# A decoder layer in float32: the token-wise projection cut into 264 and 512 columns instead of three times 256

## The chip, the cores and the metric

One core of one Trainium2 chip runs the whole layer in one launch. The metric is the device time of the launch in microseconds (us); lower is better. The median of three runs before the change is 2868.61 us.

## The reference

One layer of a hybrid decoder for 2048 tokens of width 1024, cut to what the change touches:

```python
mod = silu(c) @ ada_w + ada_b            # shift1, scale1, gate1, shift2, scale2, gate2
h = rms_norm(x) * (1 + scale1) + shift1
proj = h @ w_in                          # q 512 | k 128 | v 128 | deltanet q,k,v 1536 | beta 4 | decay 4 | z 512 | gates 2048
q, k = rope(rms_norm(q)), rope(rms_norm(k)); o_attn = sliding_window_attention(q, k, v, sinks)   # window 128
dq, dk, dv = silu(causal_conv(deltanet_qkv))                                                     # 4 taps, 12 x 128 channels
beta, g = sigmoid(beta), -exp(a_log) * softplus(decay + dt_bias)
o_dn = gated_delta_rule(l2norm(dq), l2norm(dk), dv, g, beta)                                      # then norm and silu(z)
x = x + gate1 * ((sigmoid(gA) * (o_attn @ wA) + sigmoid(gD) * (o_dn @ wD)) @ w_out)
x = x + gate2 * swiglu(rms_norm(x) * (1 + scale2) + shift2)
```

## The kernel before

The tokens are worked on in four blocks of 512 (`b` = 0 to 3); the feed-forward part runs after block 1 and after block 3 for two blocks at once. Every float32 product is made of three matmuls in the type fp32r: both operands are split into a high and a low part, and hi x hi, lo x hi and hi x lo are summed in one PSUM bank. ScalarE (ACT) makes the high part of the weights (`w_hi`, line 1074), VectorE (DVE) the low one (`w_lo`, line 1616). Both of them work through `split(b, u)`, unit of weights after unit, over a ring of three buffers, so a unit can't be split before TensorE (PE) has done with the unit three places earlier. A unit is 128 x 1024 values.

Each engine executes a sequence that is written out by hand; nothing is scheduled by a program. Semaphores tie the sequences together. Within a block the sequences run through these stages:

- *Channels.* Twelve units (`U_DN`) give the 12 x 128 deltanet channels with the weights standing and 512 tokens streaming (`by_feature`, line 2457, 24 matmuls of 512 columns). For each channel ACT empties the bank (line 1232), DVE runs the four taps (lines 1963 to 1968), ACT applies silu (line 1257). DVE's step for channel `c` is: split the unit two channels ahead, wait for the bank, four taps. Strength and decay (beta, decay; 8 columns) come from `by_group` (line 2467) after channels 0 and 1: 32 columns of plain float32 weights, laid over the four column groups of the array, so that the result lies in features by tokens and must be turned by four more matmuls with `gather8` (line 2591). `gates_1` to `gates_4` on DVE make the gates out of them during channels 2, 4, 6 and 10. In block 0 the two first channels are made while the norm delivers `h` one slice of 128 features at a time.
- *Token stage.* Queries, keys and values (768 columns) are made with tokens as the standing operand and the weights streaming, in three groups of 256 columns (`by_token`, line 2487), each in two half units. Between them, for each of the four token tiles `t`, PE runs `turn_features(t)` (lines 2622 and 2627), `key_grams(t)` (lines 2633 to 2638) and, in blocks 0 and 1 only, `modulation_product(t)` (line 2376). Then the four z units (`by_feature`). DVE runs `key_norms(t)` (lines 1984 to 1996) and `key_products(t)` (lines 2005 to 2009) for each tile; in blocks 0 and 1 it also makes one of the eight remaining pieces of the modulation per tile: `ada_sums` (lines 1604 and 1607) sums a 1024-deep product by eight operations of 128x512, `modulation` (line 1589) takes the result back.
- *Mixing.* Sixteen gate units are laid as filler between the steps of attention and of the delta rule (`fill`), then branches, output projection, feed-forward.

What PE waits for in the token stage:

```python
def turn_features(t):
    if t == 0: pe.wait_ge(silu_done.sem, ...)      # all twelve channels, and gc_ready of DVE
    else:
        pe.wait_ge(f_ready.sem, f_ready.at(b, t))  # key_products(t - 1)
        if b < 2: pe.wait_ge(ada_read, 4 + 4 * b + t)   # modulation of tile t - 1
def modulation_product(t):
    if b < 2:
        pe.wait_ge(vr_ready.sem, vr_ready.at(b, t + 1))  # key_norms(t)
        ada_product(4 + 4 * b + t)                       # waits for ada_done: ada_sums of that piece
```

Of the kernel before, what the change touches and what calls it, by code (L numbers as in the profile page):

```python
# [21 lines left out]
P = 128  # L22
# [11 lines left out]
BLK = 512  # L34
# [3 lines left out]
ATW = QKW + KV_HEADS * HEAD_DIM  # L38
DNT = 3 * DN_HEADS
# [20 lines left out]
U_DN = 0  # L60
U_AT = U_DN + DNT
U_Z = U_AT + 2 * (ATW // 256)
# [6 lines left out]
UW = 1024  # L69


J_BA = 0
J_DN = J_BA + 2
J_AT = J_DN + DNT
J_Z = J_AT + 2 * 3
# [32 lines left out]
def j_dn(c):  # L108
    return J_DN + c if c >= 2 else c


J_BOTH = J_BA + 2


def sequence():

    units, banks = [], []
    for b in range(NB):
        units += [(U_DN + c, "third bank" if c == 2 else "bank") for c in range(DNT)]
        banks += ["A"] * (2 + DNT + J_BRANCH - J_AT) + ["V"] * (J_PER - J_BRANCH)  # L120
        for i in range(3):
            units += [(U_AT + 2 * i, "half"), (U_AT + 2 * i + 1, "two banks")]
# [15 lines left out]
def last_uses():  # L138
# [3 lines left out]
    for _, kind in UNITS:  # L142
# [3 lines left out]
        else:  # L146
            j += {"bank": 1, "two banks": 2, "third bank": 3}[kind]
# [91 lines left out]
def layer_program(nc, x, cond, pos, ada_w, ada_bc, g1, g2, qkg, sinks, a_log, dt_bias, conv_w,  # L239
                  dn_g, w_ba_cols, wstream, wgate, wdown, out):  # L240
# [36 lines left out]
    proj, o = at("proj", [P, NT, ATW], fp32, o)  # L277
# [24 lines left out]
    raw_last, o = at("raw_last", [P, UW], fp32, place_z)  # L302
# [42 lines left out]
    ba_sb, _ = at("ba_sb", [P, BLK], fp32, place_d)  # L345
# [34 lines left out]
    td_raw = [at(f"td_raw{k}", [P, BLK], fp32, start + 2048 * k)[0] for k in range(6)]  # L380
# [3 lines left out]
    fw_hi, fw_lo = [[fw_both[:, part, k * FW:k * FW + FW] for k in range(PARTS)] for part in range(2)]  # L384
# [6 lines left out]
    w_ba = sb("w_ba", [P, KD, 32])  # L391
    gather8 = sb("gather8", [P, 2 * DN_HEADS])
# [68 lines left out]
    def pair(j):  # L461

        return gb[:, (j % 4) * 512:(j % 4) * 512 + 1024].rearrange("p (t n) -> p t n", t=NT)

# [56 lines left out]
    def gate_raw(b, v):  # L521

        return raw_last if v % 4 == 3 else w_raw[(U_PER * (b + 1) + v % 4) % RING]
# [31 lines left out]
    def bank_of(i, p):  # L555
# [16 lines left out]
    ba_evac, ba_turned = sig("ba_evac", 1), sig("ba_turned", 1)  # L572
# [43 lines left out]
    consts_in, cond_in, pool_set, pos_in, picks_set, picks_summed, w_ba_in = [  # L616
        nc.alloc_semaphore(s) for s in ("consts_in", "cond_in", "pool_set", "pos_in", "picks_set", "picks_summed", "w_ba_in")]
# [14 lines left out]
    out_stored = [Signal(w_ba_in, 32, 16), Signal(cond_in, 32, 16 * N_COND), Signal(consts_in, 32, 16 * N_CONSTS),  # L632
# [20 lines left out]
    with nc.Block() as block:  # L653
# [3 lines left out]
        def _(sp):  # L657
# [8 lines left out]

            def load_unit_at_once(u):
                sp.dma_start(w_raw[u][:, :], wstream[u]).then_inc(w_loaded[u], 16)
# [14 lines left out]
            sp.dma_start(w_ba[:, :, :], w_ba_cols).then_inc(w_ba_in, 16)  # L683

            def load_unit(b, u):
                sp.wait_ge(w_ready.sem, b * U_PER + (u + 1))
                s = slot(b, u)
                sp.dma_start(w_raw[s][:, :], wstream[UNITS[b * U_PER + u][0]]).then_inc(w_loaded[s], 16)
# [77 lines left out]
            for b in range(NB):  # L766
# [60 lines left out]
                def load_parts(n):  # L827
# [9 lines left out]
                    sp.dma_start(fw_both[:, :, k * FW:k * FW + FW].bitcast(fp32), park_w[n]).then_inc(parts_in[k].sem, 16)  # L837
# [212 lines left out]
        def _(act):  # L1050
# [14 lines left out]
            def split(b, u):  # L1065
# [8 lines left out]
                act.activation(w_hi[s][:, :], w_raw[s][:, :], ACT.Copy).then_inc(w_high.sem, 1)  # L1074
# [23 lines left out]
            def high(b, n):  # L1098
# [28 lines left out]
                if not be and 2 <= n < N_GATE + 2:  # L1127
                    k = part_slot(b, n - 2)
                    act.wait_ge(p_ready.sem, p_ready.at(be, n - 1))
                    act.dma_start(park_w[n - 2], fw_both[:, :, k * FW:k * FW + FW].bitcast(fp32)).then_inc(parts_out[k].sem, 16)  # L1130
# [82 lines left out]
            norm_high(N_OPEN, 0)  # L1213
            split(0, 1)
            for k in range(1, 3):
                norm_high(N_OPEN, k)
            keep_rows(2)
            norm_high(N_OPEN, 3)
            keep_rows(3)
# [1801 lines left out]
```

## Time and profile before

| | |
|---|---|
| three runs | 2867.28, 2873.40, 2868.61 us; median 2868.61 |
| profiled execution | span 2869.9 us from first to last instruction; no time of its own is listed beside it |
| PE busy | 2827.2 us (99% of the span), 14954 matmuls |
| DVE busy | 1815.7 us (63%) |
| ACT busy | 1238.8 us (43%) |
| granted TensorE clock, mean | 0.996 |
| chain that ended last | PE 85%, DVE 6%, ACT 3%, DMA 2% |

Matmuls are pipelined: a matmul is shown as busy from its issue to its modelled end, so what one costs in a run of them is the distance between two starts. The same holds for DVE and ACT, whose instructions overlap by some tens of ns; below, durations of a step are start to start. A number in square brackets at the end of a row is idle time of the engine before it, with what ended it.

### The profile page before, as it was taken

Reading aid. Unit: us, or ns where it says so; the run is one execution under the profiler, and the core shown is the slowest. Engines: PE = TensorE matmul, PEld = TensorE weight load, DVE = VectorE, ACT = ScalarE, POOL = GpSimd, SP = SyncE. Lnnn points to the kernel's source line nnn. Section 1 sums busy time; section 2 is a strip of 40 time slices with the busy share of each in tenths; the row PEclk is TensorE's granted clock in tenths of the full one; section 3 lists DMA queues with packets and bytes.
Section 4 is the critical chain, followed back from the end, with each engine's and each line's share of the span. In section 5 each row is a group of like instructions: output and inputs, shape, how many; then the busy total and the mean of one; then the engine's idle time right before and its main releaser. Section 6 shows DMA issues by size and latency. Waiting matters only on the chain.

```text
span 2869.9 us, 39887 instructions
## 1 busy us (share of the span) xinstructions
PE 2827.2 (99%) x14954; PEld 2329.4 (81%) x14954; DVE 1815.7 (63%) x3122; ACT 1238.8 (43%) x2232; POOL 133.1 (5%) x124
## 2 busy tenths in 40 slices
PE   9999999999999999999999999999999999999999
PEld 6887888977877888888889878788778888888887
DVE  5876566875687666657976666665757622223686
ACT  4554535554544333344445555355444311112343
POOL 0011000010020000000000110000100100000000
PEclk9999999999999999999999999999999999999999
DMA  7443353533448777785433334424343666677743
GB/s 303 158 140 101 129 177 117 189 101 105 161 165 317 294 290 294 291 341 192 136 119 107 120 99 137 148 89 151 81 141 122 223 239 232 242 246 265 298 135 102
DMA packets 222511, 523.51 MB, mean 182 GB/s; under 512 B 43248, under 2 KB 43504, under 8 KB 213360
## 3 DMA queue, kind: packets, MB, share of 16 engines
q1 hardware_dynamic: 173344, 423.40, 44.2%
q10 hardware_dynamic: 48976, 97.56, 9.0%
q8 instruction: 120, 1.97, 0.3%
q14 instruction: 71, 0.58, 0.1%
HBM read 362.03 MB, written 158.86 MB: 182 GB/s over the span
## 4 chain that ended last, share of the span: by engine, by line
PE 85%; DVE 6%; ACT 3%; DMA 2%; DVEq 2%; issue 1%; SPq 1%; POOL 0%; ACTq 0%
PE gb L2457 26%; PE mb L2501 22%; PE gb L2501 19%; PE gb L2882 5%; PE gb L2487 4%; PE mb L2726 2%; PE mb L2699 1%; PE mb L2721 1%; PE mb L2627 1%; ACT sc L1364 1%; DVE tmp_c L2068 1%; DVE w_lo L1616 1%; DVE inv_c L2071 1%; DMA ada_buf<-in_ada_w 1%; DVE a_mx L2052 1%
## 5 line engine op out<-in xcount | busy, mean ns | idle before, releaser
L2457 PE MATMUL gb<-h_hi,w_hi 128*128 128x512 f32 x1024 | 407.6, 398 | 3.9 <-DVE w_lo L1616 3.4
L2457 PE MATMUL gb<-h_lo,w_hi 128*128 128x512 f32 x1024 | 405.7, 396 | 0.0
L2457 PE MATMUL gb<-h_hi,w_lo 128*128 128x512 f32 x1024 | 405.7, 396 | 0.0
L2501 PE MATMUL mb<-t_hi,fw_both 128*128 128x512 f32 x1056 | 349.7, 393 | 9.6 <-DVE t_lo L1794 5.5
L1616 DVE TENSOR_TENSOR w_lo<-w_raw,w_hi 128x1024 fp32r<-128x1024 f32 x216 | 262.7, 1219 | 79.8 <-ACT w_hi L1074 78.9
L1074 ACT ACTIVATE w_hi<-w_raw 128x1024 fp32r<-128x1024 f32 x216 | 228.0, 1055 | 87.9 <-PE gb L2882 40.7
L2501 PEld LDWEIGHTS mb<-t_hi,fw_both 128*128 128x128 f32 x1056 | 199.9, 189 | 54.9 <-DVE t_lo L1794 8.1
L2457 PEld LDWEIGHTS gb<-h_hi,w_hi 128*128 128x128 f32 x1024 | 192.7, 188 | 52.9 <-issue 7.3
L2457 PEld LDWEIGHTS gb<-h_lo,w_hi 128*128 128x128 f32 x1024 | 192.8, 188 | 42.6 <-issue 4.8
L2457 PEld LDWEIGHTS gb<-h_hi,w_lo 128*128 128x128 f32 x1024 | 192.7, 188 | 39.9
L2501 PE MATMUL gb<-td_hi,fw_both 128*128 128x512 f32 x704 | 219.6, 390 | 0.3 <-DVE td_lo L1783 0.2
L2501 PE MATMUL mb<-t_lo,fw_both 128*128 128x512 f32 x528 | 206.9, 392 | 0.0
L1140 ACT ACTIVATE td_hi<-td_raw 128x512 fp32r<-128x512 f32 x154 | 96.5, 627 | 167.1 <-DMA td_raw<-scratch_hid 64.3
L2501 PE MATMUL mb<-td_hi,fw_both 128*128 128x512 f32 x528 | 163.4, 389 | 0.0
L1148 ACT ACTIVATE snap<-mb 128x512 f32<-128x512 f32 x88 | 52.4, 597 | 250.2 <-PE mb L2501 249.5
L2501 PEld LDWEIGHTS gb<-td_hi,fw_both 128*128 128x128 f32 x704 | 132.2, 188 | 28.8 <-issue 1.6
L1845 DVE TENSOR_TENSOR c_sum<-gb,snap 128x512 f32<-128x512 f32 x88 | 60.3, 687 | 148.7 <-PE gb L2501 148.2
L1783 DVE TENSOR_TENSOR td_lo<-td_raw,td_hi 128x512 fp32r<-128x512 f32 x154 | 105.7, 687 | 70.3 <-ACT td_hi L1140 70.0
L2501 PE MATMUL gb<-td_lo,fw_both 128*128 128x512 f32 x352 | 137.0, 389 | 0.0
L2501 PEld LDWEIGHTS mb<-t_lo,fw_both 128*128 128x128 f32 x528 | 99.9, 189 | 20.5
L2501 PE MATMUL gb<-t_hi,fw_both 128*128 128x512 f32 x352 | 115.4, 389 | 0.9 <-DVE t_lo L1798 0.9
L2501 PE MATMUL mb<-h_hi,fw_both 128*128 128x512 f32 x352 | 116.3, 390 | 0.0
(370 smaller groups left out, 5962.1 us busy)
## 6 DMA issues: line engine op xcount, KB each, us to landing
w_raw<-in_wstream SPq DMA_DIRECT2D x216, 512.0 KB, 3.6
scratch_parts<-fw_both ACTq DMA_DIRECT2D x154, 512.0 KB, 4.0
fw_both<-scratch_parts SPq DMA_DIRECT2D x154, 512.0 KB, 4.6
scratch_hid<-spill SPq DMA_DIRECT2D x22, 1792.0 KB, 7.4
td_raw<-scratch_hid SPq DMA_DIRECT2D x154, 256.0 KB, 2.9
ada_buf<-in_ada_w SPq DMA_DIRECT2D x24, 1024.0 KB, 7.7
w_raw<-in_wgate SPq DMA_DIRECT2D x34, 512.0 KB, 8.1
wq<-in_wdown SPq DMA_DIRECT2D x8, 1280.0 KB, 11.0
```

The lines of the kernel that those rows point to most:

```text
L1074: act.activation(w_hi[s][:, :], w_raw[s][:, :], ACT.Copy).then_inc(w_high.sem, 1)
L1140: act.activation(td_hi[step % T_RING][:, :], td_raw[k][:, :], ACT.Copy).then_inc(t_high.sem, 1)
L1148: act.activation(snap[k][i % 2][:, :], bank_of(i, p), ACT.Copy).then_inc(gate_acts.sem, 1)
L1364: last = act.activation(sc[:, h, 0:P], sc[:, h, 0:P], ACT.Copy, scale=a_sm[:, h:h + 1])
L1616: dve.tensor_tensor(w_lo[s][:, :], w_raw[s][:, :], w_hi[s][:, :].bitcast(fp32), ALU.subtract).then_inc(w_ready.sem, 1)
L1783: dve.tensor_tensor(td_lo[k][:, :], td_raw[raw_slot(step)][:, :], td_hi[k][:, :].bitcast(fp32), ALU.subtract).then_inc(t_ready.sem, 1)
L1845: dve.tensor_tensor(c_sum[k][i % 2][:, :], bank_of(i, p), other[i % 2][:, :], ALU.add).then_inc(gate_sums.sem, 1)
L2457: last = pe.matmul(bank(j), w, r, start=(i == 0), stop=(i == n - 1))
L2487: last = pe.matmul(pair(j)[:, t, :], l, w, start=first, stop=final, skip_group_check=True)
L2501: done = pe.matmul(out, w, (lo if part == 1 else hi)[:, tile, :] if tile is not None else (lo if part == 1 else hi), start=(first and part ...
L2726: last = pe.matmul(out[:, h, :], lhs(h), rhs(h), start=True, stop=True)
L2882: last = pe.matmul(bank(j), w, r, start=(k == 0 and part == 0), stop=(k == 3 and part == 2))
```

## The change

- Strength and decay columns are joined to keys and values: one product of 264 columns (`KVW`), with tokens standing, in two half units of 128 x 1056 (`wfirst`), made ahead of the channels. `by_group`, `gather8` and its four matmuls, the load of `w_ba` and ACT's copy of `ba_sb` are gone; ACT now copies 4 x 264 columns into `proj`.
- The queries are one product of 512 columns, four quarter units of two slices, worked through by `beside(count)` in steps of three matmuls, followed by the z units in the same steps (64 steps in all).
- DVE's modulation sums are cut in halves and moved: two of the four pieces of a block go into channels 3, 5, 7 and 9, the other two stay in the token stage as halves at four places.
- ACT: the query banks are emptied together (`queries_out`) behind `features(2)`; order of z and features changed.
- In the opening the split of the second unit stands behind the fourth slice of `h`.
- The weight buffers are 1056 wide; the feed-forward's halves of them are addressed by `half_unit`.

Core of the diff:

```diff
+QW = HEADS * HEAD_DIM
+TOKW = ATW + 2 * DN_HEADS
+KVW = TOKW - QW
...
+        units += [(U_KV, "half"), (U_KV + 1, "four banks")]
+        units += [(U_DN + c, "bank") for c in range(DNT)]
+        units += [(U_Q + i, "half") for i in range(3)] + [(U_Q + 3, "four banks")]
...
 # ScalarE
+                split(b, 2)
+                split(b, 3)
+                for t in range(NT):
+                    act.wait_ge(full.sem, full.at(b, J_KV + t + 1))
+                    act.activation(proj[:, t, QW:TOKW], bank(J_KV + t)[:, 0:KVW], ACT.Copy).then_inc(a_evac, 1)
...
+                features(2)
+                queries_out()
                 split(b, U_Z + 2)
+                key_decays(2)
                 act.drain()
                 squares(0)
+                features(3)
                 z_out(0)
                 split(b, U_Z + 3)
+                key_decays(3)
...
 # VectorE, channels and token stage
+                    if b < 2 and c in (3, 5, 7, 9):
+                        ada_sums(4 + 4 * b + c // 6, range(4) if c % 4 == 3 else range(4, KD))
...
+                key_norms(0)
+                split(b, U_Q + 3)
+                key_products(0)
+                modulation(4 + 4 * b)
+                key_norms(1)
+                ada_sums(6 + 4 * b, range(4))
+                split(b, U_Z)
+                key_products(1)
+                modulation(5 + 4 * b)
+                ada_sums(6 + 4 * b, range(4, KD))
+                split(b, U_Z + 1)
+                key_norms(2)
+                ada_sums(7 + 4 * b, range(4))
+                split(b, U_Z + 2)
+                key_products(2)
+                modulation(6 + 4 * b)
+                key_norms(3)
+                split(b, U_Z + 3)
+                ada_sums(7 + 4 * b, range(4, KD))
+                key_products(3)
+                modulation(7 + 4 * b)
...
 # TensorE
+            def token_product(b, u, j, t, k, width, first, hi, lo):
+                s, at_ = slot(b, u), (k - first) * width
+                for part in range(3):
+                    l = (lo if part == 1 else hi)[:, k, t * P:t * P + P]
+                    w = (w_lo if part == 2 else w_hi)[s][:, at_:at_ + width]
+                    last = pe.matmul(bank(j + t)[:, 0:width], l, w, start=(k == 0 and part == 0),
+                                     stop=(k == KD - 1 and part == 2))
...
-                by_group(b, J_BOTH, h_hi, h_lo).then_inc(full.sem, 2)
-                            last = pe.matmul(mb[:, t * 8:t * 8 + 8], ba_sb[:, t * P:t * P + P], gather8[:, :], start=True, stop=True)
...
-                token_half(U_AT, J_AT, 0)
+                beside(8)
                 for t in range(NT):
-                    u, j = U_AT + 2 * t, J_AT + 2 * t
                     turn_features(t)
-                    if t < 3:
-                        token_half(u, j, 1)
-                    else:
-                        z_unit(1)
+                    beside(6)
                     key_grams(t)
-                    if t:
-                        modulation_product(t)
-                    if t < 2:
-                        token_half(u + 2, j + 2, 0, (lambda: modulation_product(0)) if t == 0 else None)
-                    else:
-                        z_unit(2 * t - 4)
-                z_unit(3)
+                    if t == 0:
+                        beside(2)
+                    modulation_product(t)
+                    beside(2 if t == 0 else 4 if t % 2 else 5)
+                beside(8 * 2 * NT)
```

VectorE in block 0, the step of channel 7, before (w_lo is the low part of a weight unit, conv_acc the taps, line numbers are those of each kernel):

```order
L1616 TENSOR_TENSOR w_lo_57<-w_raw_51,w_hi_54 128x1024
L1963 COPY halo<-qkv 128x3
L1965 TENSOR_SCALAR conv_acc_139<-qkv,taps 128x512
L1968 SCALAR_TENSOR_TENSOR conv_acc_139<-qkv,taps,conv_acc_139 128x512 x3
```

and after the change:

```order
L1611 TENSOR_TENSOR w_lo_57<-w_raw_51,w_hi_54 128x1024
L1955 COPY halo<-qkv 128x3
L1957 TENSOR_SCALAR conv_acc_139<-qkv,taps 128x512
L1960 SCALAR_TENSOR_TENSOR conv_acc_139<-qkv,taps,conv_acc_139 128x512 x3
L1597 TENSOR_SCALAR ada_sum<-ada_buf_66,cs 128x512
L1600 SCALAR_TENSOR_TENSOR ada_sum<-ada_buf_66,cs,ada_sum 128x512 x3
L1611 TENSOR_TENSOR w_lo_55<-w_raw_49,w_hi_52 128x1024
```

Four operations of a modulation sum now stand between the taps of channel 7 and the split of the unit that PE takes two channels later.

VectorE in block 0, the end of the token stage after the change, from the modulation of tile 2 on:

```order
L1582 TENSOR_TENSOR mod_b<-mb,cbias 128x4
L1978 TENSOR_REDUCE d_ss<-t_sq 128x8
...
L1990 TENSOR_TENSOR st_vr_119<-mb,d_rt 128x512
L1611 TENSOR_TENSOR w_lo_55<-w_raw_49,w_hi_52 128x1024
L1600 SCALAR_TENSOR_TENSOR ada_sum<-ada_buf_66,cs,ada_sum 128x512 x4
L1999 SCALAR_TENSOR_TENSOR st_nt_113<-mb,g_nbr,t_dT 128x128 x4
```

The second half of the last sum stands behind the norms of tile 3 and behind a split; before, a whole sum stood ahead of the norms.

## Rows read from the trace of the kernel before

**Rows 1.** Timeline of PE, block 0: start us, us, engine, line, operation; 512- then 256-column matmuls.

```profile
99.71 0.39 PE L2457 MATMUL gb<-h_hi,w_lo 128*128 128x512 f32 x1
...
107.87 0.39 PE L2457 MATMUL gb<-h_hi,w_lo 128*128 128x512 f32 x1
108.09 0.28 PE L2487 MATMUL gb<-w_hi,h_hi 128*128 128x256 f32 x1
...
113.72 0.28 PE L2487 MATMUL gb<-w_lo,h_hi 128*128 128x256 f32 x1
```

**Rows 2.** Timeline of PE, block 0: strength and decay, and their turning.

```profile
48.10 1.92 PE L2467 MATMUL gb<-h_hi,w_ba 128*32 128x512 f32 x16
...
51.67 0.50 PE L2457 MATMUL gb<-h_hi,w_hi 128*128 128x512 f32 x1
...
57.25 0.96 PE L2591 MATMUL mb<-gather,ba_sb 128*128 128x8 f32 x8
58.06 0.47 PE L2457 MATMUL gb<-h_hi,w_hi 128*128 128x512 f32 x1
```

**Rows 3.** Timeline of PE, block 0: the opening.

```profile
29.59 0.50 PE L2457 MATMUL gb<-h_hi,w_hi 128*128 128x512 f32 x1 [1.01 <-DVE w_lo L1616]
```

**Rows 4.** Timeline of DVE, channels of block 0: one step, the gates, a wait, the last.

```profile
74.85 0.16 DVE L1722 TENSOR_SCALAR nea<-nea 128x4 f32<-128x4 f32 x1
...
76.88 1.22 DVE L1616 TENSOR_TENSOR w_lo<-w_raw,w_hi 128x1024 fp32r<-128x1024 f32 x1
78.02 0.16 DVE L1963 COPY halo<-qkv 128x3 f32<-128x3 f32 x1
...
80.97 1.22 DVE L1616 TENSOR_TENSOR w_lo<-w_raw,w_hi 128x1024 fp32r<-128x1024 f32 x1
...
98.04 0.17 DVE L1963 COPY halo<-qkv 128x3 f32<-128x3 f32 x1 [2.20 <-ACT qkv L1232]
...
111.99 0.68 DVE L2012 TENSOR_TENSOR gc_diag<-gc_full,gc_diag 16x512 fp32r<-16x512 f32 x1
```

**Rows 5.** Timeline of DVE, token stage of block 0, tile 0.

```profile
115.61 0.48 DVE L1604 TENSOR_SCALAR ada_sum<-ada_buf,cs 128x512 f32<-128x512 f32 x1
116.16 5.71 DVE L1607 SCALAR_TENSOR_TENSOR ada_sum<-ada_buf,cs,ada_sum 128x512 f32<-128x512 f32 x7
121.79 1.21 DVE L1984 TENSOR_REDUCE d_ss<-t_sq 128x8 f32<-128x1024 f32 x1
...
124.98 2.35 DVE L1616 TENSOR_TENSOR w_lo<-w_raw,w_hi 128x1024 fp32r<-128x1024 f32 x2
127.49 1.12 DVE L2005 SCALAR_TENSOR_TENSOR st_nt<-mb,g_nbr,t_dT 128x128 f32<-128x128 f32 x4 [0.16 <-issue]
...
129.73 0.15 DVE L1589 TENSOR_TENSOR mod_g<-mb,cbias 128x4 f32<-128x4 f32 x1
```

**Rows 6.** Timeline of PE, token stage of block 0: grams, modulation, turning.

```profile
121.48 0.40 PE L2633 MATMUL mb<-above,ident_r 128*128 128x512 f32 x1
...
123.42 0.36 PE L2487 MATMUL gb<-w_hi,h_hi 128*128 128x256 f32 x1
...
126.37 0.95 PE L2376 MATMUL mb<-ones,ada_sum 128*128 128x1 f32 x8
...
130.23 0.49 PE L2622 MATMUL mb<-gc_diag,rows_of 48*128 48x512 f32 x1
...
131.94 0.36 PE L2487 MATMUL gb<-w_hi,h_hi 128*128 128x256 f32 x1
```

**Rows 7.** Timeline of ACT, token stage of block 0, tile 1: features, then a split.

```profile
132.22 0.60 ACT L1295 ACTIVATE t_sq<-mb 128x512 f32<-128x512 f32 x1 [7.48 <-PE mb L2627]
...
134.66 1.11 ACT L1074 ACTIVATE w_hi<-w_raw 128x1024 fp32r<-128x1024 f32 x1
```

**Rows 8.** Timeline of PE and windows (PE busy, PEld, DVE, ACT, POOL, clock, DMA share, GB/s): idle, then lower clock.

```profile
867.29 0.47 PE L2501 MATMUL mb<-t_hi,fw_both 128*128 128x512 f32 x1 [3.18 <-DVE c_sum L1845]
...
866.00:872.00 6.00, 4.71 (x14) 3.76 (x15) 5.63 (x9) 3.79 (x7) 0.00 (x0) 0.72 0.39 144
```

More of the change, by code:

```diff
@@ L118, in sequence @@
     for b in range(NB):
[L119 to L122, printed above, removed]
+        units += [(U_KV, "half"), (U_KV + 1, "four banks")]
+        units += [(U_DN + c, "bank") for c in range(DNT)]
+        banks += ["A"] * J_BRANCH + ["V"] * (J_PER - J_BRANCH)
+        units += [(U_Q + i, "half") for i in range(3)] + [(U_Q + 3, "four banks")]
         units += [(U_Z + h, "bank") for h in range(DN_HEADS)]
@@ L146, in last_uses @@
         else:
-            j += {"bank": 1, "two banks": 2, "third bank": 3}[kind]
+            j += {"bank": 1, "two banks": 2, "four banks": 4}[kind]
             found.append(("full", j))
@@ L379, in layer_program @@
     assert o <= top[0]
-    td_raw = [at(f"td_raw{k}", [P, BLK], fp32, start + 2048 * k)[0] for k in range(6)]
+    half_unit = lambda k: k // 2 * UW + k % 2 * FW
+    td_raw = [at(f"td_raw{k}", [P, BLK], fp32, start + 4 * half_unit(k))[0] for k in range(6)]
     place_hi = start + RING * UW * 4
@@ L1212, in _ @@
             act.wait_ge(ada_read, 2)
-            norm_high(N_OPEN, 0)
-            split(0, 1)
-            for k in range(1, 3):
+            for k in range(3):
                 norm_high(N_OPEN, k)
@@ L2409, in norm_stat, with keep_warm @@
                 last.then_inc(n_stat, 1)
-            def keep_warm(j, count):
+            def keep_warm(out, count):
                 for _ in range(count):
-                    pe.matmul(bank(j)[:, 0:P], ident[:, :], ident[:, :], start=True, stop=True)
+                    pe.matmul(out, ident[:, :], ident[:, :], start=True, stop=True)
             def norm_spread(which):
@@ L2458, in by_feature @@
                 return last
-            def by_group(b, j, hi, lo):
-                pe.wait_ge(w_ba_in, 16)
-                free_bank(b, j)
-                for part in (hi, lo):
-                    for k in range(KD):
-                        rows = slice(32 * (k % GROUPS), 32 * (k % GROUPS) + 32)
-                        last = pe.matmul(bank(j)[rows, :], w_ba[:, k, :], part[:, k, :].bitcast(fp32),
-                                         start=(part is hi and k < GROUPS), stop=(part is lo and k >= GROUPS))
-                return last
@@ L2474, in by_token, with keys_half @@
+            def keys_half(b, half):
+                u = U_KV + half
                 pe.wait_ge(w_ready.sem, w_ready.at(b, u + 1))
[L2475 to L2487 removed]
@@ L2488, in by_token, with queries_part @@
-                return last
+                for t in range(NT):
+                    if half == 0:
+                        free_bank(b, J_KV + t)
+                    for k in range(4 * half, 4 * half + 4):
+                        last = token_product(b, u, J_KV, t, k, KVW, 4 * half, h_hi, h_lo)
+                    if half:
+                        last.then_inc(full.sem, 1)
+                if half == 0:
+                    last.then_inc(half_done.sem, 1)
+            def queries_part(b, part, first, count):
+                u = U_Q + part
+                if first == 0:
+                    pe.wait_ge(w_ready.sem, w_ready.at(b, u + 1))
+                for step in range(first, first + count):
+                    t, k = step // 2, 2 * part + step % 2
+                    if part == 0 and step % 2 == 0:
+                        free_bank(b, J_Q + t)
+                    last = token_product(b, u, J_Q, t, k, QW, 2 * part, h_hi, h_lo)
+                    if part == 3 and step % 2:
+                        last.then_inc(full.sem, 1)
+                    if part < 3 and step == 2 * NT - 1:
+                        last.then_inc(half_done.sem, 1)
@@ L3005 @@
         "dn_g": f(dn_norm_g).reshape(P, 1),
-        "w_ba": w_in_[:, C_BA:C_BA + 32].reshape(KD, P, 32).transpose(1, 0, 2),
+        "wfirst": np.stack([token(key_columns, h * 512, 4) for h in range(2)]),
         "wstream": np.stack(units),
```

226 lines of the change are left out of this document (99 added, 127 removed).

## The prediction

> **What bounds the kernel now.** I read the page first: PE is busy for 99% of the span and makes 85% of the chain that ended last, DVE is busy for 63%. So a matmul taken out shortens the kernel, as long as DVE, on which PE waits at a few places, can follow. Then PE's timeline, for what a matmul costs. Matmuls of 512 columns start 0.227 us apart (107.87 - 99.71 over 36), those of 256 columns 0.120 us apart (113.72 - 108.09 over 47) [rows 1]. Half the columns cost more than half the time: there is a part of about 0.013 us per matmul that doesn't depend on columns. Last, DVE's timeline, for how near it is to being late: in the channels one step is a split of 1.14 us (76.88 to 78.02) and taps of 2.95 (78.02 to 80.97), 4.09 together, and PE makes a channel in 24 x 0.227 = 5.44. DVE then waits for the next channel, 2.20 us at one place [rows 4]. That wait is the room into which half of the modulation sums now goes.
>
> **PE work taken out.** Per block: 3 x 96 matmuls of 256 columns go, 288 x 0.120 = 34.5 us. `by_group` goes, 3.57 (48.10 to 51.67), and the turning with `gather8`, 0.81 (57.25 to 58.06) [rows 2]. In their place come 96 matmuls of 264 columns; the straight line through the two spacings gives 0.123, so 11.8 us (bounds: 0.120 and 0.227, taken at the near end, since 264 is next to 256), and 96 of 512 columns, 21.8 us. 38.9 - 33.6 = 5.3 us less per block, 21.2 in all. In the opening PE sat idle for 1.01 us until the second unit was split [rows 3]; that unit is needed only at the fifth slice of `h` now: another 1.0 (bounds 0 and 1.5). The load of `w_ba` and ACT's copy lay beside other work: nothing. **22.2 us less work for PE.**
>
> The Trainium skill ("TensorE: Matmul & The Clock Gate", section "Back-to-back issue gap") gives columns / 2.4 + 2.5 ns for a warm matmul: 216, 109 and 113 ns for 512, 256 and 264. By that, regrouping the columns would gain nothing (31.4 us before, 31.5 after), the sum would be 4 us worse, and the time 2878. The trace disagrees with its fixed part, 13 ns here instead of 2.5; I go by the rows.
>
> **DVE in the channels, blocks 0 and 1.** A whole modulation sum takes 6.18 us (115.61 to 121.79), its first four operations 0.55 + 3 x 0.804 = 2.96, the other four 3.22 [rows 5]. They are behind the taps of channels 3, 5, 7 and 9: 12.4 us. From the start of the taps of channel 3 to the end of those of channel 11 DVE then has nine taps (26.6), eight splits (9.1), the sums (12.4), 2.0 for the second gate step with the scales beside it (74.85 to 76.88) [rows 4], about 0.8 each for the third and fourth, of three to five instructions of the same kind, and 0.1 for a copy: 51.8 us (51.5 in block 1, without scales). PE gives it eight channels, 43.5, about 0.9 of small products behind channel 8, and the last taps 2.95: 47.4. So DVE ends 4.4 and 4.1 late, wherever on the way PE starts to wait for a split. The slack at the end is small: before, the last step of DVE ahead of `turn_features(0)` ended at 112.7 (111.99 + 0.68) [rows 4], and PE had filler until 113.8 [rows 1], 1.1 us; the filler is 5.44 long now instead of 5.8, which leaves 0.8. **PE waits 3.6 and 3.3 us, 7 in all**, most of it ahead of the first `turn_features`. In blocks 2 and 3 there are no sums, and DVE has its 1.3 us per channel to spare: no wait.
>
> **DVE in the token stage, blocks 0 and 1.** Durations: turning 1.7 (130.23 to 131.94), grams 1.9 (121.48 to 123.42), modulation product 0.8, a filler step 3 x 0.227 = 0.68 [rows 1, 6]; squares of tile t ready 3.1 after the turning's start (2.0 to the first, 1.1 for both), features done on ACT 4.4 after it (134.66 - 130.23) [rows 6, 7]; norms 3.2 (121.79 to 124.98), products and modulation 2.4 (127.49 to 129.9) [rows 5]; 0.2 for each hand-over. All times from the start of `turn_features(t)`:
> - Tile 0: PE is through at 11.5, DVE at about 10.7. No wait.
> - Tile 1: DVE 3.1 + norms 3.2 + half sum 3.0 + split 1.1 + 2.4 + 0.2 = 13.0. PE 1.7 + six steps 4.1 + 1.9 + 0.8 + four steps 2.7 = 11.3. **Wait 1.7.**
> - Tile 2: DVE begins with the other half sum and a split, 4.4, then 3.2 + 3.0 + 1.1 + 2.6 = 14.3. PE 11.9 (five steps behind the grams) and 0.5 for a bank: after four steps, at 4.5, z needs the bank of the first queries, and ACT comes to it behind `features(2)`, at 4.4 + 0.6. **Wait 1.9.**
> - Tile 3: the last half sum stands behind norms (6.3) and a split, whose high part ACT makes behind features, a table load, the first z and itself (about 7.4); split until 8.6, sum until 11.9. PE asks for it at 1.7 + 4.1 + 1.9 = 7.7. **Wait 4.1.** Before, a whole sum was in front of the norms, so this order is new.
>
> That is 7.7 us in each of two blocks, 15.4, and the bank's 0.5 in all four, 2.0. What is behind the waiting matmul on PE is filler that nobody waits for but that has to be done. Where DVE is ahead of PE afterwards nothing comes back: the mixing stage is PE's own.
>
> **The clock.** After an idle time of 3.18 us the granted clock was 0.5: in the six microseconds around it the mean is 0.72, that is 3.4 us at the lower of the two levels, and 1.7 us lost [rows 8]. I expect four waits of over 3 us: two at the first turning (3.3 to 3.6) and two at the last modulation product (4.1). I charge it to the two longer ones, 3.4 us, with ends of 0 and 6.8.
>
> **Sum:** -22.2 + 7 + 15.4 + 2.0 + 3.4 = **+5.6 us**. The profiled span is 2869.9, 1.3 over the median of the three runs and within their spread; the sum is a difference and I set it on the median: 2868.6 + 5.6 = **2874.2 us**.
>
> **Rivals.**
> - *DVE keeps up* (the other side). DVE's total is only 63% of the span; if PE's waits overlap and ACT's order leaves no more than the banks' 2.0, the time is 2868.6 - 22.2 + 2.0 = 2848.4. It decides as soon as DVE's lag at channel 11 is under 0.8 us and the last sum is done at 7.7. Against it: the lag is a plain sum of measured steps, 4 us over. Chance 0.12.
> - *Half of the waits.* Some of my hand-overs are too long, or a sum slips into a gap; 12 us of waits and no clock loss: 2859. Chance 0.15.
> - *Waits as worked out, the clock stays up*, or the waits are a fifth shorter: 2864 to 2874. Chance 0.33, which is the case within 0.2%.
> - *The forecast, and more*: clock lost once to four times, 2874.3 to 2884. Chance 0.34. With all four it is 2877.6. The Trainium skill (same page, section "Part 1: The HAM clock gate") says that the low clock is the default state and that activity lifts it, which would make every long wait cost. The trace agrees for the wait of 3.18 us [rows 8].
> - *The part of a matmul that doesn't depend on columns is nearly nothing where the product is made*, so that regrouping gains nothing and only `by_group`, the turning and the opening are won: 4 us more, 2878. The rows of both widths speak against it [rows 1]. Chance 0.04. The gap rule of the Trainium skill named above would give this case.
> - *264 columns don't run like 256*: at 0.227 each, 384 x 0.104 = 40 us more, 2914. Nothing in the rows speaks for it, and so the change would not do what it says. Chance 0.02.
>
> **The numbers.** What a measurement of this kernel can tell from no change is about 0.2%, 5.7 us: faster is below 2862.9, slower above 2874.3. My forecast lies on the upper edge. Faster 0.27, within 0.33, slower 0.40. The range from 2854 to 2883 leaves out the first rival, the last one and a few per cent above.
>
> **What would show it.** Right: 384 matmuls of 264 columns 0.123 apart; idle on PE at the first `turn_features` of blocks 0 and 1, released by DVE or ACT (the last taps and silu), of 3 to 4 us; idle at the modulation product of tile 3, released by `ada_sum`, of about 4; both absent in blocks 2 and 3, which are each 5 us shorter than before; waits of PE on DVE some 22 us longer in total. Wrong: PE's idle time about as before, which would give the first rival; or a spacing of the 264 columns far from 0.123; or waits elsewhere, such as for a weight unit that lands late.

## The result and the profile after

The changed kernel takes 2918.12 us, median of four runs (2914.48 to 2919.31); the kernel before, run beside it, 2869.3. The ratio is 1.0158, with a 95% interval of 1.0146 to 1.017: **slower by 1.6%, 45 us**, where I had forecast 2874.2 and a range up to 2883. The profiled run took 2914.48.

The head of the page, and the granted clock. PE is busy for 98% (99% before), with 14,410 matmuls, and the mean clock is that of before, 0.996.

```profile
span 2912.5 us, 38783 instructions
...
PE 2852.8 (98%) x14410; PEld 2310.6 (79%) x14410; DVE 1816.3 (62%) x3121; ACT 1230.6 (42%) x2240; POOL 133.4 (5%) x124
```
```profile
core 0: 2912.5 us, clock 0.996
```

PE's timeline, the new product of 264 columns: two matmuls, the second 22 steps behind the first, to set beside [rows 1].

```profile
29.91 0.28 PE L2476 MATMUL gb<-w_hi,h_lo 128*128 128x264 f32 x1
...
32.59 0.28 PE L2476 MATMUL gb<-w_lo,h_hi 128*128 128x264 f32 x1
```

(32.59 - 29.91) / 22 = 0.122 us. That was forecast (0.123), and the idle time of [rows 3] is gone.

PE's waits, summed by line and releaser: us in total, times, longest. These six groups stand nowhere in the answer for the kernel before.

```profile
PE mb L2386 <- issue: 7.9, 2, 4.0
...
PE mb L2630 <- DVE gc_diag L2006: 5.3, 2, 2.7
...
PE mb L2630 <- DVE mod_g L1582: 2.9, 2, 1.6
PE gb L2467 <- ACT proj L1278: 2.0, 4, 0.5
...
PE mb L2630 <- DVE mod_a L1582: 1.3, 1, 1.3
PE mb L2630 <- DVE mod_b L1582: 1.1, 1, 1.1
```

And where they lie in block 0, on PE's timeline (in brackets the idle time before the matmul): the first turning, two later turnings, and the modulation product of tile 3. Below them two rows of DVE ahead of that product, a split and the last half sum, to set beside [rows 5].

```profile
122.78 0.46 PE L2630 MATMUL mb<-gc_diag,rows_of 48*128 48x512 f32 x1 [2.73 <-DVE gc_diag L2006]
...
147.81 0.46 PE L2630 MATMUL mb<-gc_diag,rows_of 48*128 48x512 f32 x1 [1.30 <-DVE mod_g L1582]
...
162.08 0.46 PE L2630 MATMUL mb<-gc_diag,rows_of 48*128 48x512 f32 x1 [1.06 <-DVE mod_b L1582]
...
169.53 1.23 DVE L1611 TENSOR_TENSOR w_lo<-w_raw,w_hi 128x1024 fp32r<-128x1024 f32 x1 [1.03 <-ACT w_hi L1072]
...
170.85 3.23 DVE L1600 SCALAR_TENSOR_TENSOR ada_sum<-ada_buf,cs,ada_sum 128x512 f32<-128x512 f32 x4
...
174.18 1.84 PE L2386 MATMUL mb<-ones,ada_sum 128*128 128x1 f32 x8 [3.97 <-issue]
```

The half sum ends at 174.08, and the product starts at 174.18: "issue" stands for that sum. The new waits are 7.9 + 5.3 + 2.9 + 2.0 + 1.3 + 1.1 = 20.5 us. With the 22.2 us that I had forecast PE to be spared, the kernel should be 2 us quicker. It is 43 us longer in the profiled runs, so some 44 us are in no wait and in no added matmul. Most of them show in the spacing of matmuls (the time from one start to the next): two matmuls of 512 columns of the channel product, 24 steps apart.

```profile
70.15 0.39 PE L2467 MATMUL gb<-h_hi,w_hi 128*128 128x512 f32 x1
...
75.73 0.39 PE L2467 MATMUL gb<-h_hi,w_hi 128*128 128x512 f32 x1
```

5.58 / 24 = 0.2325 us. In the kernel before it was 0.227 [rows 1], at the same granted clock. From the start times of all matmuls of both traces, the mean of the spacings under 300 ns, by the line that issues them (of the kernel before), and their count:

```
512-column matmuls of              count   before   after   difference x count
the channels, z, gates (L2457)      3840    228.0   232.0    15.4 us
the feed-forward part (L2501)       5544    226.8   232.0    28.8 us
the branches (L2882)                 768    230.3   232.3     1.5 us
```

That is 46 us. The 512-column matmuls of the channels, z, gates and the feed-forward part cost 4 to 5 ns more each, those of the branches 2, although the change touches few of these instructions. The extra time differs by weight buffer. The median spacings of the channel product in the changed kernel, from one of its three products to the next (ns):

```
buffer of the ring            0     1     2     (before: 226 to 227 in each)
h_hi,w_hi -> h_lo,w_hi       227   233   227
h_lo,w_hi -> h_hi,w_lo       232   233   232
h_hi,w_lo -> h_hi,w_hi       234   235   234
```

One thing in the change reaches all of these (what follows was an inference at this point; the experiments test it): its nine weight buffers (three each of `w_raw`, `w_hi`, `w_lo`) are 1,056 columns wide, 4,224 bytes in a partition where they had 4,096, and everything behind them in SBUF is moved by 9 x 128 = 1,152 bytes. Before, all these addresses were equal modulo 256. Now, counted from the start of the ring, the three `w_hi` stand at 128, 0, 128 modulo 256, the three `w_lo` at 0, 128, 0, and `h_hi`, `h_lo`, the operands that stream, at 128. Call an address modulo 256 bytes its phase. In the table a step is at 227 where both matmuls have a `w_hi` of the same phase as `h`, and slow wherever a standing operand with another phase is in it.

### The profile page after: what moved, and what is told of

It is laid out like the page before. It is cut to its first block, busy times and chain, and to the rows that moved or that the text cites. A ratio compares the mean times of both kernels' runs of the same rounds, so it can differ in the third digit from the quotient of the medians.

```text
span 2912.5 us, 38783 instructions
## 1 busy us (share of the span) xinstructions
PE 2852.8 (98%) x14410; PEld 2310.6 (79%) x14410; DVE 1816.3 (62%) x3121; ACT 1230.6 (42%) x2240; POOL 133.4 (5%) x124
## 4 chain that ended last, share of the span: by engine, by line
PE 81%; DVE 9%; ACT 3%; DVEq 3%; issue 2%; DMA 2%; SPq 1%; POOL 0%; ACTq 0%
PE gb L2467 23%; PE mb L2520 22%; PE gb L2520 19%; PE gb L2899 5%; PE gb L2476 3%; PE mb L2743 2%; DVE conv_acc L1960 1%; DVE ada_sum L1600 1%; PE mb L2716 1%; DVE w_lo L1611 1%; PE mb L2738 1%; PE mb L2635 1%; DVE tmp_c L2078 1%; DVE inv_c L2081 1%; DVEq L1959 1%
## 5 line engine op out<-in xcount | busy, mean ns | idle before, releaser
L2467 PE MATMUL gb<-h_hi,w_lo 128*128 128x512 f32 x1024 | 412.5, 403 | 0.0
L1611 DVE TENSOR_TENSOR w_lo<-w_raw,w_hi 128x1024 fp32r<-128x1024 f32 (+1 forms) x216 | 263.4, 1221 | 94.2 <-ACT w_hi L1072 93.6
L1072 ACT ACTIVATE w_hi<-w_raw 128x1024 fp32r<-128x1024 f32 (+1 forms) x216 | 228.2, 1057 | 102.2 <-PE gb L2899 42.1
```

Source lines behind the costliest of these rows:

```text
L1072: act.activation(w_hi[s][:, 0:width], w_raw[s][:, 0:width], ACT.Copy).then_inc(w_high.sem, 1)
L1611: dve.tensor_tensor(w_lo[s][:, 0:width], w_raw[s][:, 0:width], w_hi[s][:, 0:width].bitcast(fp32), ALU.subtract).then_inc(w_ready.sem, 1)
L2467: last = pe.matmul(bank(j), w, r, start=(i == 0), stop=(i == n - 1))
```

## The experiments

**Theory A**: a 512-column matmul is slower when its standing operand (the weights) and its moving one (the tokens) differ in their address modulo 256. **Rivals**: B, any move of the buffers does it; C, the wider transfers, or what contends with them; D, the width of the buffers itself; E, the absolute address. The address needs no other change to be tested: a gap between the weights and the tokens does it in the kernel before. Here and below, "in the kernel before" means that nothing else differs.

### A gap of 256, 128 and 64 bytes, and a common shift

In the kernel before, one line ahead of the tokens' buffers (128; in the others 256 and 64), and in the fourth one line ahead of everything:

```diff
+    top[0] += 128
     zone1 = top[0]
```
```diff
+    start += 128
     size = {fp32: 4, fp32r: 4, i8: 1, i32: 4}
```

256 bytes:

> The kernel before, with 256 bytes left free between the weight buffers and the buffers of the normalized tokens, so that every moving operand of zone 1 and behind stands 256 bytes further on. Theory A (a 512-column matmul starts 6 ns later when its standing and its moving operand differ in their byte address modulo 256): nothing differs modulo 256, spacing 227 ns, 2869 us. Rival B (any shift of the zones from the weight ring, or the room that is filled, changes the time): above 2869, up to the changed kernel's 2918. Rival C (the change's cost comes from its 1056-column transfers and what contends with them): 2869, since no transfer changes.

128 bytes:

> The kernel before with 128 bytes left free at the same place, and nothing else. Theory A (modulo 256): all weight buffers now differ from the moving operands by 128 modulo 256, so all three products of each split weight are slow: spacing 233 to 235 ns in place of 227 on all 512-column matmuls that read zone 1 and the zones behind it; some 10,000 such matmuls by 6 to 8 ns are 60 to 80 us, hence 2929 to 2949 us. With a weaker mismatch (only part of the operands are hit) at least the changed kernel's +45. Rival C (transfers, contention): 2869, spacing 227, because the transfers are those of before. Rival D (the width of the buffers, 1056 columns, is what counts and not the phase): 2869.

64 bytes:

> The same with 64 bytes. If the phase counts in steps of 128 bytes or more: either 2869 (64 is inside the step) or as with 128; if it counts by 64 bytes or finer (theory A with a finer grain): slow as with 128 bytes, 2915 to 2949. Rivals C and D: 2869.

All by 128 bytes:

> The kernel before with everything, weight buffers and moving operands alike, 128 bytes further on. Theory A (the difference of the two operands counts): 2869, spacing 227. Rival E (the absolute address of an operand counts, a multiple of 256 or more being quick): slow on all 512-column matmuls, 2930 and above.

Measured, with the ratio to the kernel before (2872.83) and its interval: 256 bytes 2873.57 us, 0.9999 (0.999 to 1.0008); **128 bytes 2914.76 us, 1.0145 (1.0129 to 1.0162)**; 64 bytes 2895.75 us, 1.0082 (1.0067 to 1.0097); all shifted 2871.32 us, 0.9998 (0.9989 to 1.0007). PE's timeline of each in this order (256, 128, 64, shift), two channel matmuls 24 steps apart:

```profile
70.26 0.39 PE L2458 MATMUL gb<-h_lo,w_hi 128*128 128x512 f32 x1
...
75.70 0.39 PE L2458 MATMUL gb<-h_lo,w_hi 128*128 128x512 f32 x1
```
```profile
70.14 0.39 PE L2458 MATMUL gb<-h_lo,w_hi 128*128 128x512 f32 x1
...
75.71 0.40 PE L2458 MATMUL gb<-h_lo,w_hi 128*128 128x512 f32 x1
```
```profile
70.08 0.39 PE L2458 MATMUL gb<-h_hi,w_lo 128*128 128x512 f32 x1
...
75.58 0.39 PE L2458 MATMUL gb<-h_hi,w_lo 128*128 128x512 f32 x1
```
```profile
70.10 0.39 PE L2458 MATMUL gb<-h_hi,w_hi 128*128 128x512 f32 x1
...
75.54 0.39 PE L2458 MATMUL gb<-h_hi,w_hi 128*128 128x512 f32 x1
```

The spacings are 5.44 / 24 = 0.227, 5.57 / 24 = 0.232, 5.50 / 24 = 0.229 and 0.227. A gap of 128 bytes with no instruction changed makes the kernel as slow as the change did; 256 bytes do nothing, and neither does the shift of both operands together. That ends B, C, D and E as causes of this effect: the difference of the two addresses counts. I had expected more of the 128 bytes (2929 to 2949): the spacing grew by 5 ns, not by 6 to 8. For the 64 bytes I had named no cost in between, only none or that of 128. Their launch costs more than half of what 128 bytes cost (+24 and +42 us by the ratios), but the spacing only a third: over all 512-column matmuls its mean is 227.5 ns before, 229.3 with 64 bytes and 232.8 with 128. With 64 bytes that is 18 us, of which the 256-column matmuls give 5 back (115.8 ns for 119.9); the rest of the profiled run's excess is 5 us of idle time of PE and 6 us of lost clock (its mean clock is 0.994, that of the kernel before 0.996). Why those came with it is not shown.

The trace of the kernel before held a case of the effect all along. Its `oA`, the attention branch's output, stands 128 bytes off the weights modulo 256, `oD`, the delta branch's, 0 bytes; both are multiplied by the same kind of weights at one line. Groups of instructions by line: busy us, mean ns of one; first the kernel before, then with the gap of 128 bytes, which sets `oA` right and `oD` wrong.

```profile
L2882 PE MATMUL gb<-oA_hi,w_hi 128*128 128x512 f32 x128 | 50.8, 397 | 0.0
...
L2882 PE MATMUL gb<-oD_hi,w_hi 128*128 128x512 f32 x128 | 49.9, 390 | 0.0
```
```profile
L2883 PE MATMUL gb<-oD_hi,w_hi 128*128 128x512 f32 x128 | 50.5, 394 | 0.0
...
L2883 PE MATMUL gb<-oA_hi,w_hi 128*128 128x512 f32 x128 | 50.3, 393 | 0.0
```

The ends of matmuls are modelled, so the start times are the better measure. Median spacings of the three kinds of step, `oA` 232, 232 and 237 and `oD` 227, 227 and 227 in the kernel before; `oA` 227, 227 and 227 and `oD` 231.5, 231.5 and 237 with the gap. They changed places, which the mean durations (394 and 393 with the gap) show only in part.

### The layout of the change without the change

The kernel before with its nine weight buffers 1,056 columns apart, the transfers and splits 1,024 columns as ever (seventeen small gate tensors of 64 bytes go into the gaps, so that the total grows by 64 bytes and not by 1,152):

```diff
+ROOM = 1056
...
-    w_hi = [sb(f"w_hi{s}", [P, UW], fp32r) for s in range(RING)]
+    w_hi = [sb(f"w_hi{s}", [P, ROOM], fp32r) for s in range(RING)]
```

> The kernel before, its units 1,024 columns as ever, with its nine weight buffers 1,056 columns apart as in the change (the gate tensors stand in the gaps); no instruction, transfer or order differs. Theory A (the layout alone costs the unforeseen time): 2912 to 2920 us, with 512-column spacings of 227 to 235 ns that differ by buffer as in the changed kernel. Rival (the layout only costs together with the 1,056-column transfers or the new order): 2869 to 2873.

Measured: 2913.3 us, **1.0149 (1.0134 to 1.0165)**, 42.8 us more. The median spacings by buffer are those of the changed kernel to within 1 ns (227, 233, 227; 232, 233, 233; 234, 235, 234). The layout alone is nearly the whole difference.

### The change without its layout

The changed kernel with its weight buffers 1,088 columns apart (4,352 bytes, 17 x 256); what is loaded and split stays 1,056 columns for the first two units and 1,024 for the others, and the gate tensors go into the gaps here too. Then the same with 128 bytes ahead of the tokens.

```diff
-UW = 4 * KVW
+KV_UNIT = 4 * KVW
+UW = 1088
...
-    return UW if u < U_DN else RAW
+    return KV_UNIT if u < U_DN else RAW
```

> The changed kernel with its nine weight buffers 1,088 columns apart in place of 1,056 (4,352 bytes, a multiple of 256), the transfers still 1,056 columns and 1,024; the seventeen small gate tensors stand in the gaps. Theory A (the change's unforeseen cost is the address phase between weights and tokens): all 512-column matmuls are back at 227 ns, the waits of the changed kernel (about 20 us) and its saving (-22.2 us) stay: 2867 to 2872 us, 46 to 50 below the changed kernel. Rival C (wider transfers, or the token-major order, slow the matmuls): 2918 as before.

With the gap:

> The aligned changed kernel with 128 bytes ahead of the token buffers, so that all weights differ from the moving operands by 128 modulo 256. Theory A: as before with 128 bytes, some 42 to 47 us above the aligned one, less what a slower TensorE hides of its waits and clock losses: 2910 to 2930. Rival (the aligned kernel is only quick because of the gaps or where the gate tensors stand): 2883.

Measured: aligned **2883.29 us, 1.0044 (1.0031 to 1.0056)**, with the gap 2925.11 us, 1.0186 (1.0172 to 1.02). The spacing is back, here (75.51 - 70.07) / 24 = 0.227:

```profile
70.07 0.39 PE L2469 MATMUL gb<-h_lo,w_hi 128*128 128x512 f32 x1
...
75.51 0.39 PE L2469 MATMUL gb<-h_lo,w_hi 128*128 128x512 f32 x1
```

Theory A holds again, but the aligned kernel isn't at 2867 to 2872: it is 12.6 us above the kernel before. The waits are those of the changed kernel (8.1, 5.6, 2.9, 2.0, 1.3 and 1.1, 21.0 in all). In the profiled run more clock is lost as well. Mean clock of the aligned kernel, then the windows (PE busy, PEld, DVE, ACT, POOL, clock, DMA share, GB/s) of the opening, of tile 3 in block 0, of that in block 1, and of the first 600 us:

```profile
core 0: 2886.1 us, clock 0.992
```
```profile
20.00:35.00 15.00, 14.78 (x84) 12.05 (x85) 7.09 (x14) 4.58 (x7) 1.02 (x1) 0.66 0.97 385
...
170.00:190.00 20.00, 15.96 (x70) 13.46 (x69) 11.30 (x22) 9.89 (x17) 1.89 (x2) 0.83 0.15 37
...
575.00:590.00 15.00, 10.98 (x48) 9.27 (x47) 8.75 (x15) 5.61 (x9) 0.56 (x1) 0.77 0.14 45
...
0.00:600.00 600.00, 567.06 (x3134) 464.63 (x3134) 407.87 (x770) 288.87 (x522) 35.34 (x49) 0.97 0.46 157
```

The same windows of the changed kernel:

```profile
20.00:35.00 15.00, 14.19 (x121) 10.48 (x120) 8.77 (x15) 5.92 (x8) 1.02 (x1) 1.00 0.98 390
...
170.00:190.00 20.00, 16.03 (x63) 13.18 (x63) 12.10 (x23) 6.32 (x10) 1.95 (x1) 0.83 0.32 105
...
575.00:590.00 15.00, 15.00 (x61) 12.20 (x62) 7.79 (x17) 3.10 (x4) 1.96 (x1) 0.89 0.34 107
...
0.00:600.00 600.00, 570.46 (x3170) 463.23 (x3171) 410.00 (x776) 293.38 (x528) 35.39 (x49) 0.99 0.48 160
```

Added up over the span, duration x (1 - clock), the clock lost is 11.3 us in the kernel before, 11.3 in the changed one, 24.2 in the aligned one and 21.1 in the aligned one with the gap. Each of these is one execution, and the loss differs from run to run of one kernel: the five runs of the aligned kernel have mean clocks of 0.992 to 0.995 and take 2888.05 to 2880.84 us. The profiled one is the slowest of them, so its account belongs beside its own span, which is 16.2 us above that of the kernel before (2886.1 and 2869.9). The account by the forecast saving is -22.2 + 21.0 + (24.2 - 11.3) = +11.7 us, 4.5 short. The traces say where most of that is: all idle time of PE (gaps of over 0.15 us) is 22.8 us more than before, the clock lost outside of it 11.8 more, and what remains of the span, PE's own work, 18.5 less. In the three versions of the next section it is 17.9 to 19.5 less. The forecast for this part was 21.2.

Blocks 2 and 3 have no sums on DVE, and there the forecast of 5 us less per block can be read alone. PE's timeline, the first matmul of block 2 and the first of the feed-forward part behind block 3, in the kernel before and in the aligned one:

```profile
1461.68 0.39 PE L2457 MATMUL gb<-h_hi,w_hi 128*128 128x512 f32 x1
...
2232.08 0.39 PE L2501 MATMUL mb<-h_hi,fw_both 128*128 128x512 f32 x1
```
```profile
1486.99 0.28 PE L2478 MATMUL gb<-w_hi,h_hi 128*128 128x264 f32 x1
...
2246.76 0.39 PE L2522 MATMUL mb<-h_hi,fw_both 128*128 128x512 f32 x1
```

770.4 and 759.8 us: 5.3 less for each block, of which 0.9 is clock that the kernel before lost there beyond what this one did. In the changed kernel with its slower matmuls it is 2.4 (765.6 for both).

Where the granted clock is low, it is at the lower of the two levels, 1.2 GHz, for some microseconds. The waits at tile 3 cost both kernels clock, in the changed one 20 x 0.17 + 15 x 0.11 = 5.1 us; the opening cost it in the aligned one alone. That the changed kernel lost no more in all than the kernel before comes from other places: three losses in the profiled run of the kernel before (in the opening, near 868 and near 1673 us, 6.8 us together) are absent from its profiled run, and one of 1.7 us near 268 is new. Whether the change or chance moved those is not shown.

### Moving the sums

Where do the waits come from? Three versions of the aligned kernel. Token stage alone, in blocks 0 and 1 (the same is done for the half sums of tiles 1 and 2, and the split of the second z unit goes behind `key_norms(2)`):

```diff
                     modulation(6 + 4 * b)
+                if b < 2:
+                    ada_sums(7 + 4 * b, range(4, KD))
                 key_norms(3)
                 split(b, U_Z + 3)
-                if b < 2:
-                    ada_sums(7 + 4 * b, range(4, KD))
```

> The aligned changed kernel with, in the token stage of the first two blocks, the modulation sums put ahead of the key norms of tiles 1, 2 and 3 and not behind them, so that the norm of the next tile isn't what the products wait for, and one weight split after the norm. If the waits of about 8 us at the modulation product (2 by 4.0) are what the traces say, they go, and nothing takes their place: 2860 to 2864 us. Rival: the time only moves to the wait of the next bank or to the grams (2868 to 2872, no gain).

Channel stage alone:

```diff
-                    if b < 2 and c in (3, 5, 7, 9):
-                        ada_sums(4 + 4 * b + c // 6, range(4) if c % 4 == 3 else range(4, KD))
+                    if b < 2:
+                        for piece, first, last in {0: ((0, 0, 2),), 1: ((0, 2, 4),), 2: ((0, 4, 5),), 3: ((0, 5, 7),),
+                                                   5: ((0, 7, 8), (1, 0, 1)), 6: ((1, 1, 2),), 7: ((1, 2, 4),),
+                                                   8: ((1, 4, 5),), 9: ((1, 5, 7),), 11: ((1, 7, 8),)}.get(c, ()):
+                            ada_sums(4 + 4 * b + piece, range(first, last))
```

> The aligned changed kernel with the pieces of one or two sums in the channel stage alone, the token stage as in the change. If the two stages' waits are separate terms, the 8 us at the modulation product stay and those of the first turns (8.5 us in all) go in part: 2870 to 2876 us, with some of the lost clock. Rival (the channel stage's lag does not matter, the token order is all): 2881 to 2885; rival (the lag of the channels feeds the token stage's waits): below 2868.

Both:

> The same, and in the channel stage the modulation sums cut into pieces of one or two operations, one piece behind nearly every channel, where the change has four pieces of four. If DVE's lag in the channels comes from pieces that are longer than its spare time in one channel, the rest of the waits (at turn_features and at the bank, 8 to 12 us) goes: 2848 to 2856 us, faster than both kernels. Rival (DVE has no spare time at all in this stage, and the lag is only the sum of its work): 2858 to 2864, as with the token order alone.

Measured: token stage 2870.42 us, 0.9993 (0.9984 to 1.0002); channel stage 2872.72 us, 1.0009 (0.9999 to 1.0018); **both 2859.47 us, 0.9962 (0.995 to 0.9975)**. PE's waits at the turnings and at the modulation product in these three, in this order:

```profile
PE mb L2631 <- DVE gc_diag L2008: 5.7, 2, 2.9
...
PE mb L2631 <- DVE mod_b L1584: 1.1, 1, 1.1
...
PE mb L2631 <- DVE mod_g L1584: 1.1, 1, 1.1
```
```profile
PE mb L2391 <- issue: 8.1, 2, 4.0
...
PE mb L2635 <- DVE mod_g L1584: 2.9, 2, 1.6
PE mb L2635 <- DVE gc_diag L2011: 2.2, 1, 2.2
...
PE mb L2635 <- DVE mod_a L1584: 1.3, 1, 1.3
PE mb L2635 <- DVE mod_b L1584: 1.1, 1, 1.1
```
```profile
PE mb L2634 <- DVE gc_diag L2011: 2.2, 1, 2.2
...
PE mb L2634 <- DVE mod_g L1584: 1.1, 1, 1.1
PE mb L2634 <- DVE mod_b L1584: 1.1, 1, 1.1
```

The two stages are separate: each edit takes its own waits and leaves the other's. The token order takes 11 us of them, the pieces in the channels 3.4. In the profiled runs the lost clock, summed as above, goes from 24.2 to 13.9 us with the token order, to 22.2 with the pieces, and to 8.6 with both; the median over all runs of the mean clock goes from 0.993 to 0.994, 0.995 and 0.996, where 0.001 is 2.9 us. So a wait taken out was worth more than its length here. How much of that is clock is uncertain by some microseconds, since the eleven runs of the token order alone lie between 0.992 and 0.996. I had expected 8 us of the token order, which brought 13, and 7 to 13 of the pieces, which brought 10 to 11. The times on record for the token order and for both edits (2860 to 2864, 2848 to 2856) were missed from above, since they started from an aligned kernel at 2867 to 2872. Together the edits are 24 us below the aligned kernel, and 0.4% quicker than the kernel before.

The same two edits in the changed kernel as it is, with its layout:

> The changed kernel as it is, weight buffers 1,056 columns apart, with the sums of both stages moved as in the quickest version. If the address phase and the waits are separate terms, the 24 us between the aligned kernels with and without the moved sums hold here less what the lost clock makes of them (12 us less was lost here than in the aligned one): 2894 to 2906 us. Rival (with a slower TensorE DVE keeps up, so the waits are worth little): 2910 to 2918.

Measured: 2901.91 us, 1.0095 (1.008 to 1.0111), 18 us less than the changed kernel by the two ratios (0.0158 - 0.0095). The same edits were worth 24 us in the aligned kernel, so layout and waits are separate terms only in part. In the profiled runs PE's idle time fell by 12.5 us here and by 15.0 there, and the lost clock not at all here (11.3 to 13.7) and by 15.5 there.

### The attention outputs set right too

```diff
-    place_v = zone4 + 16512
+    place_v = zone4 + 16640
...
-    qT, o = at("qT", HW, fp32, zone4 + 24736)
+    qT, o = at("qT", HW, fp32, zone4 + 24864)
```

> The quickest version so far (aligned, both stages' sums moved) with the attention outputs oA, which stand 128 bytes off the weights in every kernel here, moved 128 bytes on; the scores behind them too. Theory A: the 384 matmuls with oA as moving operand go from 232 to 237 ns to 227, like those with oD: 384 by 5 to 8 ns are 2 to 3 us, hence 2856 to 2858 us, at the edge of what can be measured; the spacings decide. Rival: the spacing of oA has another reason (its producers, or the place in the stage), and stays at 232: 2859 to 2860.

Measured: **2858.49 us, 0.9946 (0.9934 to 0.9959)**. The intervals of this kernel and of the one without the edit overlap, so its time shows no gain. The spacings do: `oA` at medians of 227 in all three kinds of step, as forecast. The groups of the kernel with the edit:

```profile
L2903 PE MATMUL gb<-oA_hi,w_hi 128*128 128x512 f32 x128 | 50.2, 392 | 0.0
...
L2903 PE MATMUL gb<-oD_hi,w_hi 128*128 128x512 f32 x128 | 49.8, 389 | 0.0
```

This is the quickest version: 15 us below the kernel before, and some 60 below the change as made.

## Why the prediction was wrong

**The step that failed** is one that I did not write as a step. The sum took the spacing of [rows 1], 0.227, for all 512-column matmuls of the new kernel, and priced only the instructions that come, go or move. The widening of `UW` from 1,024 to 1,056 columns was read as a size of two transfers. It moved the phase of nearly every operand, and some 10,000 matmuls became 4 to 5 ns longer: 46 us, eight times the whole forecast difference. In launch time the layout alone cost 42.8 us by the ratios, and 32.7 on top of the aligned change (45.3 - 12.6), with 12.9 us less of lost clock in the changed kernel's profiled run than in the aligned one's.

**PE work taken out, 22.2.** The mechanism holds, the size is some 3 us too large: the 264 columns are 0.122 apart (0.123 forecast), the opening's idle time of 1.0 is gone, and blocks 2 and 3 are 5.3 us shorter in the aligned kernel, but PE's work is 17.9 to 19.5 us less in the four aligned kernels of the last sections, not 21.2. A part of it, 0.8 us, is in the 384 matmuls of the queries, 229.0 apart on average where I had 227; the rest is open. The gap rule of the Trainium skill ("TensorE: Matmul & The Clock Gate", section "Back-to-back issue gap"), which would have made 264 columns 113 ns, is not what these rows show (122).

**DVE in the channels, 7.** 5.3 at the first turnings, 2.73 and 2.57 by block where I had 3.6 and 3.3. The mechanism was right: it is the first `turn_features` that waits, in blocks 0 and 1 alone, and smaller pieces take 3.4 of 5.6 us away in the aligned kernel.

**DVE in the token stage, 15.4.** 13.2: at tile 3, 4.0 in each block (4.1 forecast); for tiles 1 and 2 of both blocks together 5.3 (7.2), at the next turning, where the sum had put them. **The bank, 2.0**: 2.0, four times up to 0.5.

**The clock, 3.4 with ends of 0 and 6.8.** I charged it to the two waits at tile 3, and there it fell, for 5.1 us in the changed kernel. The balance with the kernel before is about 0 all the same, since losses elsewhere are absent; in the aligned kernel's profiled run it is +12.9, in the opening and at the first turning of block 0 too. What a mean clock does from run to run was not in the sum. The rival of more lost clock, up to 2884, has the aligned kernel's time, 2883.29, but not its parts: the saving was smaller than it assumed, and the clock was not lost at the four long waits alone.

So for the change without its layout the forecast of +5.6 stands against +12.6: 2883.29 measured beside a kernel before at 2872.36, which is 2881 on the 2868.6 of the forecast, near the upper end of the range (2883). That it fell inside is partly luck, since the saving was too large by 3 us and the waits as a whole 3 us too long in the forecast (24.4 for 21.0); for the change as made the range was wrong, since none of its cases had a cost outside the edited stages. The rival with the largest time, 2914, came near the measured number by chance, and its mechanism is excluded by the 264-column rows.

## What to carry to other kernels

A change of a buffer's size is a change of the address of everything behind it: write down the addresses of the standing and moving operands of the big matmuls before and after, modulo 256, and keep them equal; if they can't be, price some 5 ns for each 512-column matmul, as measured here for fp32r. Read the spacing of matmuls from their starts, separately for each pair of operands: medians of 232 and 237 for one operand and 227 for another at one line were a sign that was there before any experiment. The mean durations alone aren't enough: 397 and 390 here, but 392 and 389 in the quickest version, where both operands are aligned. And put work that fills an engine's spare time ahead of what waits anyway, in pieces no longer than the spare time, since the place of the half sums was worth as much as the regrouped columns.

## What the runs showed of the hardware

A matmul of 512 fp32r columns starts 227 ns after the one before it when the weights and the tokens are equal modulo 256 bytes in their partitions, 229 to 230 ns at a difference of 64 bytes, 232 ns (for some steps 237) at 128, and 227 again at 256. Shifting both does nothing. Where `w_hi` and `w_lo` also differ from each other it is up to 235. The 256-column matmuls, which have tokens standing and weights moving, don't become slower: medians of 120 ns in the kernel before, 118.5 to 120 with 128 bytes, 117 with 64. The roles are not the reason: the queries of the changed kernel are 512 columns wide with tokens standing, and their medians for the three kinds of step go from 227, 227 and 229 in the aligned kernel to 231, 231 and 232 with the gap of 128 bytes. Which two accesses get in each other's way is not shown; differences other than 64, 128 and 256 bytes were not tried. The Trainium skill ("SBUF — State Buffer", section "Operand start alignment") lets an operand start at any multiple of its element size and says of this that it is "about legality, not speed"; all the addresses here are legal by it, and the runs supply the speed.
